# Feed-forward in four token blocks of 5, 4, 4 and 4 tiles in place of three of 6, 6 and 5

## The reference, cut to what matters

```python
def conv_ffn(h, conv_hist, w_up, w_dw, b_dw, w_down):
    up = h @ w_up                                    # 1024 -> 2 * 2816
    T = up.shape[1]
    ext = jnp.concatenate([conv_hist.astype(up.dtype), up], axis=1)
    c = ext[:, 0:T] * w_dw[0] + ext[:, 1:T + 1] * w_dw[1] + ext[:, 2:T + 2] * w_dw[2] + b_dw
    a, b = jnp.split(c, 2, axis=-1)
    return (jax.nn.silu(a) * b) @ w_down, ext[:, -(CONV_W - 1):]
...
    x2 = layer_norm(ALPHA * x1 + ffn + ple, ln2_g, ln2_b)
```

## Time and profile before

| | us |
|---|---|
| median of three runs | 3122.96 |
| the profiled execution, its own time | 3125.76 |
| its span, first to last instruction | 3123.9 |
| PE busy in the span (matmuls, overlapping ends counted once) | 2948.6 |
| POOL, DVE, ACT busy | 1399.9, 1612.0, 1358.4 |
| the feed-forward, first matmul to the end of the span | 1543.9 to 3123.9 |

### The profile page before, as it was taken

One profiled execution on the slowest core, in us unless ns is written; L12 is line 12 of the kernel. 1 busy time (PEld: TensorE's weight loads), 2 busy tenths in 40 slices (PEclk: granted clock), 3 DMA queues, 4 the chain that ended last, 5 costly groups with the idle time before them and its releaser, 6 DMA issues.

```text
span 3123.9 us, 43638 instructions
## 1 busy us (share of the span) xinstructions
PE 2948.6 (94%) x15336; PEld 2585.6 (83%) x15336; DVE 1612.0 (52%) x2178; ACT 1358.4 (43%) x2635; POOL 1399.9 (45%) x830
## 2 busy tenths in 40 slices
PE   6997898999999799999699999999999999999997
PEld 5776776777777578888599999999999999999996
DVE  3453686767767444444244444365444436544446
ACT  4332554767777522221243334344333434544443
POOL 5232553666656632222144344384434338544444
PEclk9998798999999899999899999999999999999999
DMA  4224554111122332222422121133212123322221
GB/s 128 68 77 63 175 171 112 33 42 42 42 50 84 104 108 86 86 89 86 153 85 73 54 67 58 63 123 127 74 54 67 54 67 115 128 81 74 74 81 59
DMA packets 162489, 263.60 MB, mean 84 GB/s; under 512 B 48496, under 2 KB 90192, under 8 KB 161200
## 3 DMA queue, kind: packets, MB, share of 16 engines
q1 hardware_dynamic: 162384, 262.27, 27.4%
...
## 4 chain that ended last, share of the span: by engine, by line
PE 49%; DVE 1%; POOL 0%; DMA 0%; ACT 0%; issue 0%; SPq 0%; DVEq 0%; POOLq 0%
PE ff_u L84 11%; PE ff_u L85 11%; PE ff_u L86 11%; PE ff_d L84 5%; PE ff_d L85 5%; PE ff_d L86 5%; DVE ff_y L2450 0%; DMA ff_x_raw<-scratch_x_t 0%; DVE ff_y L2499 0%; DVE ff_stats L2482 0%; POOL ff_y L2285 0%; POOL ff_w_lo L2235 0%; POOL ff_rstd L2275 0%; DVEq L2073 0%; ACT ff_w_hi L2307 0%
## 5 line engine op out<-in xcount | busy, mean ns | idle before, releaser
L2235 POOL TENSOR_TENSOR ff_w_lo<-ff_w_raw,ff_w_hi 128x1024 fp32r<-128x1024 f32 x198 | 520.9, 2657 | 732.4 <-ACT ff_w_hi L2307 732.4
L84 PE MATMUL ff_u<-ff_x_hi,ff_w_hi 128*128 128x384 f32 (+1 forms) x2112 | 689.1, 326 | 21.1 <-POOL ff_w_lo L2235 21.1
L86 PE MATMUL ff_u<-ff_x_lo,ff_w_hi 128*128 128x384 f32 (+1 forms) x2112 | 688.8, 326 | 0.0
L85 PE MATMUL ff_u<-ff_x_hi,ff_w_lo 128*128 128x384 f32 (+1 forms) x2112 | 688.6, 326 | 0.0
L84 PEld LDWEIGHTS ff_u<-ff_x_hi,ff_w_hi 128*128 128x128 f32 x2112 | 398.4, 189 | 22.8 <-POOL ff_w_lo L2235 21.5
L85 PEld LDWEIGHTS ff_u<-ff_x_hi,ff_w_lo 128*128 128x128 f32 x2112 | 398.4, 189 | 1.1
L86 PEld LDWEIGHTS ff_u<-ff_x_lo,ff_w_hi 128*128 128x128 f32 x2112 | 398.3, 189 | 0.0
L2429 DVE SCALAR_TENSOR_TENSOR ff_cv_a<-ff_up_a,ff_taps,ff_cv_a 128x768 f32<-128x768 f32 (+1 forms) x132 | 155.3, 1176 | 348.9 <-ACT ff_cv_a L2356 340.9
L2450 DVE TENSOR_TENSOR ff_y<-ff_y,ff_d 128x512 f32<-128x512 f32 x374 | 239.6, 681 | 146.3 <-PE ff_d L86 146.2
L84 PE MATMUL ff_d<-ff_w_hi,ff_h_hi 128*128 128x512 f32 x748 | 291.3, 389 | 4.4 <-DVE ff_y L2450 4.4
L85 PE MATMUL ff_d<-ff_w_hi,ff_h_lo 128*128 128x512 f32 x748 | 291.5, 390 | 0.0
...
## 6 DMA issues: line engine op xcount, KB each, us to landing
...
```

Of the source, the lines that this page charges most:

```text
L84: pe.matmul(out, lh, rh, start=first, stop=False, **kw)
L85: pe.matmul(out, ll, rh, start=False, stop=False, **kw)
L86: return pe.matmul(out, lh, rl, start=False, stop=last, **kw)
L2235: pool.tensor_tensor(w_lo[:, slot], w_raw[:, n % RAWS, :].rearrange("p (k c) -> p k c", c=P), f32(w_hi[:, slot]), ALU.subtract).then_inc(w ...
```

## The change

`BLOCKS` becomes (5, 4, 4, 4), and everything that named three blocks counts `NB` of them. A block of four tiles has 512 columns, so its up products are one chunk, and the four up banks then hold two sets: an even `f` uses `ps_u[0]` and `ps_u[2]`, an odd one `ps_u[1]` and `ps_u[3]`. PE's `rows` waits for the evacuation of `f - 2` there. The block of five tiles keeps two chunks, now 320 + 320. Buffers that were 768 columns wide are 640. All 66 weight units are loaded and split four times in place of three. The sample tokens stay in the last block.

```diff
-BLOCKS = (6, 6, 5)
-FIRST = (0, 6, 12)
+BLOCKS = (5, 4, 4, 4)
+NB = len(BLOCKS)
+FIRST = (0, 5, 9, 13)
 BW = BLOCKS[0] * P
-CHW = BW // 2
...
         def chunks(b):
 
             w = BLOCKS[b] * P
-            return (0, CHW), (CHW, w - CHW)
+            return ((0, 0, w // 2), (1, w // 2, w // 2)) if w > 512 else ((1, 0, w),)
+
+        def up_bank(b, f, s, c):
+
+            return ps_u[2 * s + (c if len(chunks(b)) == 2 else f % 2)]
...
-            for b in range(3):
+            for b in range(NB):
...
-                    for c, (a, w) in enumerate(chunks(b)):
-                        ps = ps_u[2 * s + c]
+                    for c, a, w in chunks(b):
+                        ps = up_bank(b, odd, s, c)
...
-                               bias=taps[:, s, at_f, 3:4]).then_inc(evac, 1)
+                               bias=taps[:, s, at_f, 3:4]).then_inc(evac, 2 // len(chunks(b)))
...
-                    for c, (a, w) in enumerate(chunks(b)):
-                        pe.wait_ge(evac, per_f(b, f - 1, 4, 2 * s + c))
+                    for c, a, w in chunks(b):
+                        back = 3 - len(chunks(b))
+                        pe.wait_ge(evac, per_f(b, f - back, 4, 2 * s + c))
                         for k in range(KD):
-                            mm = part(b, s, c, a, w, k, slots)
-                        mm.then_inc(upped, 1)
+                            mm = part(b, s, c, a, w, k, slots, odd)
+                        mm.then_inc(upped, 2 // len(chunks(b)))
```

More of the change, by code:

```diff
@@ L2130, in chunks @@
             w = BLOCKS[b] * P
[L2131 removed]
+            return ((0, 0, w // 2), (1, w // 2, w // 2)) if w > 512 else ((1, 0, w),)
+        def up_bank(b, f, s, c):
+            return ps_u[2 * s + (c if len(chunks(b)) == 2 else f % 2)]
         def prompt_w(b):
[L2134 removed]
+            return BLOCKS[b] * P - (SAMPLE if b == NB - 1 else 0)
         def sample_rows(buf):
[L2138 removed]
+            at0 = 2 + prompt_w(NB - 1)
             return buf[:, at0:at0 + ROWS * (NEW + 2)].rearrange("p (r t) -> p r t", t=NEW + 2)
@@ L2199, in _ @@
                     load_w(b, n)
-            sp.wait_ge(carried, per_f(2, FT - 1, 2, 1) + 2 * FT)
+            sp.wait_ge(carried, per_f(NB - 1, FT - 1, 2, 1) + 2 * FT)
             sp.dma_start(g["conv_p"].rearrange("p (s f) t -> p s f t", s=2), carry[:, :, :, :]).then_inc(st_c, 16)
@@ L2203, in _ @@
               .then_inc(st_c, 16)
-            store_y(2)
+            store_y(NB - 1)
             sp.wait_ge(st_y, 16 * TT)
@@ L2265, in pair @@
                     weight(b, n0 + n, base, slot)
-                if last and b < 2:
+                if last and b < NB - 1:
                     opening(b + 1, (0, 1), (0, 1))
@@ L2296, in _ @@
                 pair(b, LAST, 4, 6 * (LAST - 1), last=True)
-            normalise(2)
+            normalise(NB - 1)
         @block.scalar
@@ L2330, in centre, with rows @@
                                    bias=offset[:, t:t + 1]).then_inc(centred, 1)
-            def rows(b, f):
+            def rows(b, f, odd):
                 pw = prompt_w(b)
@@ L2375, in pair @@
                     f = 2 * p + i
-                    rows(b, f)
+                    rows(b, f, i)
                     act.wait_ge(conv, per_f(b, f, 4, 1))
@@ L2388, in pair @@
                             weight(b, n0 + n, 0, slot, q2)
-                    if last and i == 1 and b < 2:
+                    if last and i == 1 and b < NB - 1:
                         opening(b + 1, (0, 1), (0, 1))
@@ L2405, in _ @@
                 pair(b, LAST, 4, 2 * (LAST - 1), last=True)
-            centre(2)
+            centre(NB - 1)
         @block.vector
@@ L2430, in convolve @@
                                                       ALU.mult, ALU.add)
-                        if b == 2:
+                        if b == NB - 1:
                             rows = cv[s][:, pw:pw + SAMPLE].rearrange("p (r t) -> p r t", t=NEW)
@@ L2490, in normalise @@
                 T = BLOCKS[b]
-                late = T if b < 2 else 2
+                late = T if b < NB - 1 else 2
                 dve.wait_ge(ln_in, 32)
@@ L2512, in _, with rows @@
             pe.sem_inc(down, BLOCKS[0])
-            def rows(b, f, n, slots, opening=False):
+            def rows(b, f, n, slots, odd, opening=False):
                 if opening:
@@ L2529, in rows, with part @@
                     for s in range(2):
-                        for c, (a, w) in enumerate(chunks(b)):
-                            mm = part(b, s, c, a, w, k, slots)
+                        for c, a, w in chunks(b):
+                            mm = part(b, s, c, a, w, k, slots, odd)
                             if k == KD - 1:
-                                mm.then_inc(upped, 1)
-            def part(b, s, c, a, w, k, slots):
-                return product(pe, ps_u[2 * s + c][:, 0:w], (w_hi[:, slots[s], k, :], w_lo[:, slots[s], k, :]),
+                                mm.then_inc(upped, 2 // len(chunks(b)))
+            def part(b, s, c, a, w, k, slots, odd):
+                return product(pe, up_bank(b, odd, s, c)[:, 0:w], (w_hi[:, slots[s], k, :], w_lo[:, slots[s], k, :]),
                                (x_hi[:, k, a:a + w], x_lo[:, k, a:a + w]), k == 0, k == KD - 1)
@@ L2555, in downs @@
                     mm.then_inc(down, 1)
-            for b in range(3):
-                rows(b, 0, 0, ODD, opening=True)
-                rows(b, 1, 2, DOWN)
+            for b in range(NB):
+                rows(b, 0, 0, ODD, 0, opening=True)
+                rows(b, 1, 2, DOWN, 1)
                 with pe.Fori(0, LAST - 1) as q:
                     n = 6 * q + 4
-                    rows(b, 2 * q + 2, n, EVEN)
+                    rows(b, 2 * q + 2, n, EVEN, 0)
                     downs(b, q, n + 2)
-                    rows(b, 2 * q + 3, n + 4, ODD)
+                    rows(b, 2 * q + 3, n + 4, ODD, 1)
                 n = 6 * (LAST - 1) + 4
-                rows(b, 2 * LAST, n, EVEN)
-                rows(b, 2 * LAST + 1, n + 4, ODD)
+                rows(b, 2 * LAST, n, EVEN, 0)
+                rows(b, 2 * LAST + 1, n + 4, ODD, 1)
                 downs(b, LAST - 1, n + 2)
```

6 lines of the change are left out of this document (2 added, 4 removed).

## The result

The changed kernel takes 3132.68 us (median of six runs, 3128.66 to 3137.37), the one before 3120.47 in six runs, the three named above among them: a ratio of 1.0038 with a 95% interval of 1.0024 to 1.0052. It is slower, by 12 us; 3132.5 was predicted. The profiled execution took 3128.66 us (span 3126.9). What comes ahead of the feed-forward differs by up to 12 us between executions, so from here on I compare the feed-forward alone, from its first matmul to the end of the span: 1590.6 us now, 1580.0 before, +10.6.

The account below looks back on a forecast made before the run. PE bounds the feed-forward at full clock, so matmul cost and waits of PE count. -14.1 + 1.5 + 5.1 + 18.1 - 1 = +9.6 us on 3122.96 gives 3132.5 us, range 3118 to 3146.

Parts of the forecast that it names:

- Fewer matmuls: Feed-forward up products: 1056 fewer matmuls, each with 13.3 ns fixed cost, save 14.1 us on PE's path.
- One more wait for additions: At the added block end, PE's last down products wait for DVE's additions a fourth time: +1.5 us.
- Inside a block: In four-tile blocks, `h_lo` takes 10.0 to 10.3 of the covering row's 10.88 us: no wait, cost nothing.
- The last pairs: Last pair of three four-tile blocks: second row waits 1.7 us for its first ODD weight's split, +5.1 us.
- The turns: At three block changes, PE waits for split weights before row 2 and `h_lo` before first down products: +18.1 us (12 to 24).
- D + 49.9: Turn between four-tile blocks: first `h_lo` 49.9 us after last down products can start, against PE's 43.5; 6.4 us waiting.
- Step 1: At a turn, the last `h_lo` ends 12.5 us after the old block's last row (E), when additions are done.
- rival C: Behind each turn's second wait PE's clock halves, losing 1.7 us three times: +5, 3137.6 us; chance 0.17.
- Start and tail: Smaller activation pieces at the start and one tile less in the last block's tail: 0 to -1.8, taken as -1 us.
- Rival A: POOL's chains a quarter shorter, so no turn waits and last-pair waits nearly go: 3110.5 us; chance 0.13.
- D (waits in every pair): In three four-tile blocks' pairs, the `h_lo` chain outlasts its cover: 8 to 13 us more, 3143 us; chance 0.12.
- Rival B: At turns, unit 6 lands early and the second wait vanishes, 18.1 becoming some 8: 3122.5 us; chance 0.13.

Follow-up runs that it names:

- e1: Changed kernel with the four-tile blocks' up products as 2 x 256 columns in one bank set, four weight passes kept: 3169.78 us, ratio to before 1.0155.
- e5: Changed kernel with the last pair's second up row's weights loaded and split ahead of the preceding down product's: 3134.56 us, ratio to before 1.0033.
- e12: Changed kernel with turn loads, splits and ln_b additions reordered, the down products' addition waits narrowed, last-pair units in PE's order: 3128.69 us, ratio to before 1.0016.
- e3: Changed kernel with the next block's first four activation pieces loaded before its first three weight units at each turn: 3133.04 us, ratio to before 1.0028.
- e4: Changed kernel with weight unit 6 loaded before the finished block's stores, units 7 and 8 before y: 3127.46 us, ratio to before 1.0022.
- e13: Changed kernel with units 6 and 7 loaded before the stores, 8 before y, and units 4 to 7 split earlier by ScalarE: 3137.86 us, ratio 1.0044.
- e14: Changed kernel with y double-buffered, LayerNorm moved to the next block's pairs 1 and 2, and loads, splits, addition waits and last pair edited: 3118.65 us, ratio 0.9992.

## Why the prediction was right

The terms came nearly as predicted. That the time came within 0.2 us is luck: I had +9.6 us on 3122.96 for the kernel before; its six runs have 3120.47, and the difference is +12.2 in the medians and +10.6 in the feed-forward.

- *Fewer matmuls, -14.1.* Right: 226.7 ns in the stream, and 42.6 us back for 3168 more matmuls in e1, 13.4 ns each. The 2.5 ns of the Trainium skill ("TensorE: Matmul & The Clock Gate", section "Wait — 56ns, not 53.3ns?") would make that 8 us, an estimate from that page; the trace doesn't bear it out.
- *One more wait for additions, +1.5.* 1.6.
- *Inside a block, nothing.* Right: `h_lo` ends 10.3 us behind its row in blocks 1 and 2 and 10.0 in block 3, of 10.88. The cover that is left is 0.6 to 0.9 us, as worked out.
- *The last pairs, +5.1.* 4.5, in three blocks, for the unit named. The work I priced there was real, but e5 and e12 show that the price was not the pair's own: without these waits the turns get longer. Terms that I had added up are not independent.
- *The turns, +18.1.* 20.2, by other parts, and that the sum is near is partly luck: the waits before row 2 and at the first down products, which were to make up all of it, came to 9.5 us (at row 2, where I had 2.9 at a turn from four tiles to four, 0.8, none and 0.6). From the last down product D to the first `h_lo` I had D + 49.9; the profile has 2409.50 - 2361.05 = 48.4. The additions ended at D + 29.2 (29.6 predicted). Over the three turns PE lost 14.3 us from D to the first down product, 4.4 of them at half clock; 3.1 came ahead of D, and 2.8 behind the first down product of the turn 0 to 1. Two steps failed in size. Step 1 had the last `h_lo` at E + 12.5, at the moment when the additions are done anyway; it came at 14.8 in block 1, because of the activation pieces that are loaded behind three weight units (e3 loads them first, and at both turns only the wait for additions is left): 3.1 us over two turns that I had not counted. And the clock: I gave rival C 0.17 as a case by itself, with three stretches of 1.7 us; it came as part of the forecast, 7.2 us in three stretches (by the brackets of the rows, 2.8 behind a wait of 3.04, 2.9 behind 3.82, 1.5 behind 2.25), while the waits of 1.94 and 2.68 left PE at 1.00. In part it replaced waits, since a slow PE is one that comes later to the next wait: the row-2 wait of turn 1 to 2 (2.9 predicted) is absent there.
- *Start and tail, -1.* -0.6, behind the last matmul.
- *The mechanism of the turns.* Half right. I had followed one chain, through VectorE's additions and the DMA of unit 6. ScalarE did wait for unit 6 at two turns of three; without these waits (e4) one wait of PE fell, by 1.3 us, and half clock went with it. None of the other orders tried cuts the rest: in ten orders, the changed kernel's among them, the turn 1 to 2 stayed between 59.5 and 64.9 us, and only the removal of the LayerNorm work (with early splits, which alone, in e13, gave nothing) brought it to 56.4. That the two engines exclude each other is read from the lengths of their instructions; an experiment with that alone was not made, and LayerNorm was not moved without the other edits of e14, the loads ahead of the stores among them. So what holds up the first `h_lo` in the changed kernel is shown only as far as this bundle: it goes when the LayerNorm work and the stores leave the turn.

Rival A (the covers hold) and D (waits in every pair) are refuted by the waits listed: all are at block ends. Rival B falls too: ScalarE did wait for unit 6 at two turns, and where it didn't, at the turn 2 to 3, and in e4, which brings the unit early, first-down waits of 1.9 us and more stay.
